# Last stage of a decoder layer: product and addition by token halves, four accumulator pairs in turn, an early root

## The reference

```python
h = h + merged @ w_out                                   # two attention branches, gated
n2 = rmsnorm(h, g_mlp)
h = h + square(relu(n2 @ w_ff1)) @ w_ff2
n3 = rmsnorm(h, g_ple)
h = h + sigmoid(n3 @ w_ple_gate) * (p @ w_ple)           # w_ple: 256 x 1024
return rmsnorm(h, g_final)                               # x * rsqrt(mean(x*x) + 1e-6) * g
```

## Time and profile before

| | |
|---|---|
| median of 3 runs | 1815.67 us (1814.73 to 1817.26) |
| profiled execution, its own time | 1816.49 us |
| its span in the trace | 1814.5 us |
| PE, share of the span | 95% |
| DVE, ACT, POOL | 45%, 31%, 20% |
| mean granted TensorE clock | 0.977 of full speed |

### The profile page before, as it was taken

One profiled execution on the slowest core, in us unless ns is written; L12 is line 12 of the kernel. 1 busy time (PEld: TensorE's weight loads), 2 busy tenths in 40 slices (PEclk: granted clock), 3 DMA queues, 4 the chain that ended last, 5 costly groups with the idle time before them and its releaser, 6 DMA issues.

```text
span 1814.5 us, 21898 instructions
## 1 busy us (share of the span) xinstructions
PE 1727.2 (95%) x8728; PEld 1364.4 (75%) x8728; DVE 808.7 (45%) x1319; ACT 559.5 (31%) x817; POOL 355.5 (20%) x166
## 2 busy tenths in 40 slices
PE   5899989999899999999998999999999999999996
PEld 4568778787556666678887888888888888888885
DVE  7499999901245576554324312122212121215334
ACT  5422322222355566621222212111211111224223
POOL 2212342123100000212211222222222222222220
PEclk8999999999899999999999999999999999999997
DMA  4202123242100020013321111111111111111112
GB/s 149 79 24 58 35 70 99 87 123 65 47 1 1 1 71 1 1 70 139 128 81 35 47 47 47 56 48 46 46 46 46 58 46 46 46 46 41 52 47 92
DMA packets 90324, 103.08 MB, mean 57 GB/s; under 512 B 15920, under 2 KB 82480, under 8 KB 90256
## 3 DMA queue, kind: packets, MB, share of 16 engines
q1 hardware_dynamic: 87504, 92.70, 16.3%
q10 hardware_dynamic: 2592, 9.44, 1.4%
q0 software_dynamic: 160, 0.02, 0.1%
HBM read 86.54 MB, written 13.76 MB: 55 GB/s over the span
## 4 chain that ended last, share of the span: by engine, by line
PE 90%; DVE 4%; ACT 3%; issue 1%; POOL 1%; DMA 0%; ACTq 0%; DVEq 0%; POOLq 0%
PE ps L1466 73%; PE ps L1684 3%; PE ps L1698 3%; PE ps L1649 2%; PE ps L1668 2%; PE ps L1655 2%; PE ps L1563 2%; PE ps L1763 1%; DVE prob_a L1296 1%; DVE sc L1167 1%; PE ps L1625 1%; DVE prob_b L1296 1%; PE ps L1494 0%; PE ps L1827 0%; POOL w_lo L652 0%
## 5 line engine op out<-in xcount | busy, mean ns | idle before, releaser
L652 POOL TENSOR_TENSOR w_lo<-w_raw,w_hi 128x1024 fp32r<-128x1024 f32 x131 | 316.4, 2417 | 1114.4 <-ACT w_hi L736 1114.4
L736 ACT ACTIVATE w_hi<-w_raw 128x1024 fp32r<-128x1024 f32 x131 | 138.7, 1061 | 928.2 <-PE ps L1466 882.0
L1466 PE MATMUL ps<-n_hi,w_hi 128*128 128x512 f32 x1120 | 350.9, 395 | 23.4 <-DVE n_lo L1365 6.6
L1466 PE MATMUL ps<-n_lo,w_hi 128*128 128x512 f32 x1120 | 349.3, 393 | 0.0
L1466 PE MATMUL ps<-n_hi,w_lo 128*128 128x512 f32 x1120 | 348.0, 392 | 0.0
L1466 PEld LDWEIGHTS ps<-n_hi,w_hi 128*128 128x128 f32 x1120 | 212.5, 190 | 71.1 <-issue 11.1
L1466 PEld LDWEIGHTS ps<-n_lo,w_hi 128*128 128x128 f32 x1120 | 213.1, 190 | 44.8
L1466 PEld LDWEIGHTS ps<-n_hi,w_lo 128*128 128x128 f32 x1120 | 212.7, 190 | 44.9
L1394 DVE TENSOR_TENSOR h<-h,ps 128x2048 f32<-128x2048 f32 x32 | 73.2, 2288 | 221.6 <-PE ps L1466 221.6
L1180 DVE TENSOR_SCALAR_CACHE_REDUCE tested<-sc,bar_i 128x384 bf16<-128x384 f32 (+2 forms) x192 | 169.0, 943 | 1.7 <-POOL sc L667 0.6
L1466 PE MATMUL ps<-hid_lo,w_hi 128*128 128x512 f32 x512 | 157.6, 389 | 0.0
(11 more groups left out here) (260 smaller groups left out, 2032.2 us busy)
## 6 DMA issues: line engine op xcount, KB each, us to landing
w_raw<-in_w_ff_dram SPq DMA_DIRECT2D x64, 512.0 KB, 3.5
w_raw<-in_w_in_dram SPq DMA_DIRECT2D x28, 512.0 KB, 3.7
gates_scratch<-stage ACTq DMA_DIRECT2D x16, 512.0 KB, 2.7
sig_ab<-gates_scratch SPq DMA_DIRECT2D x8, 1024.0 KB, 5.9
x_tok<-in_x_dram SPq DMA_DIRECT2D x8, 512.0 KB, 10.5
w_raw<-in_w_out_dram SPq DMA_DIRECT2D x8, 512.0 KB, 4.8
xs<-in_x_dram SPq DMA_DIRECT2D x4, 1024.0 KB, 5.1
w_raw<-in_w_ple_gate_dram SPq DMA_DIRECT2D x8, 512.0 KB, 3.4
```

What stands on the lines that cost most here:

```text
L652: pool.tensor_tensor(w_lo[s][:, :, :], w_raw[s][:, :, :], w_hi[s][:, :, :].bitcast(F32), ALU.subtract).then_inc(lo_ready, 1)
L736: act.activation(w_hi[s][:, :, :], w_raw[s][:, :, :], ACT.Copy).then_inc(hi_ready, 1)
L1466: last = pe.matmul(bank(4 * half + 2 * j + t)[0:w, :], wm, xm[:, t * HALF:(t + 1) * HALF], start=(k == 0 and a), stop=(k == total - 1 and ...
```

## The change

- The product and the addition of round q = 3 are made for tokens 0 to 511 and then for tokens 512 to 1023, four instructions instead of two. `h_final` counts both halves, and PE waits only for the first before it turns tiles 0 to 3, and for the second before tile 4. Between the first product and its addition stands a wait of DVE on its own semaphore (`link`).
- The transposes of tile t go to `fin_bank(t)`: all eight banks as four pairs in turn. Tiles 0 to 3 wait for the two halves to be free of earlier groups, later tiles for the final product of tile t - 4, which a new semaphore `fin_out` counts.
- The output has four buffers, `fin_stage(t)`, both slots of `tmp`, with four `stored` semaphores. The columns of the root are four too, `fin_c`, in the place of `max_c`.
- ACT's squares go to a place of their own, `squares`, over `n2_hi`.
- Right behind the last Sigmoid ACT takes the root of the column `eps_c` into `fin_c[:, 0:1]`, which nothing reads.

```diff
@@ storage and helpers
+        squares = at("squares", NX + 32 * K, [2, S])
+        fin_c = max_c
-        stored = [sem("stored0"), sem("stored1")]
+        stored = [sem(f"stored{b}") for b in range(4)]
+        def fin_bank(t):
+            return bank(4 * ((FIN_GROUP + (t // 2) % 2) % 2) + 2 * (t % 2), 2)
+
+        def fin_stage(t):
+            return tmp[:, (t // 2) % 2, t % 2, :]
@@ SP
             for t in range(TT):
-                g = FIN_GROUP + t
-                freed(sp, g % 2, free_count(g))
-                sp.dma_start(out2[t * P:(t + 1) * P, :], tmp[:, t % 2, 0, :]).then_inc(stored[t % 2], 16)
+                sp.wait_ge(fin_out, t + 1)
+                sp.dma_start(out2[t * P:(t + 1) * P, :], fin_stage(t)).then_inc(stored[t % 4], 16)
@@ ACT
+            act.activation(fin_c[:, 0:1], eps_c, ACT.Sqrt).then_inc(fin_ss, 1)
             for t in range(TT):
-                half = group()
-                if t >= 2:
-                    freed(act, half, free_count(FIN_GROUP + t - 2))
-                act.activation(tmp[:, t % 2, 1, :], bank(4 * half, 2), ACT.Square,
+                group()
+                act.activation(squares[:, t % 2, :], fin_bank(t), ACT.Square,
                                accum_out=ss_c[:, t % 2:t % 2 + 1]).then_inc(fin_ss, 1)
-                act.wait_ge(fin_ss, t + 1)
-                act.activation(rstd_c[:, t % 2:t % 2 + 1], ss_c[:, t % 2:t % 2 + 1], ACT.Sqrt,
+                act.wait_ge(fin_ss, t + 2)
+                act.activation(fin_c[:, t % 4:t % 4 + 1], ss_c[:, t % 2:t % 2 + 1], ACT.Sqrt,
                                bias=eps_c, scale=1.0 / D).then_inc(fin_std, 1)
@@ DVE
                 half = group(1)
-                gate = tmp[:, q % 2, :, :].rearrange("q a n -> q (a n)")
-                pair = h[:, 2 * q:2 * q + 2, :].rearrange("q a n -> q (a n)")
                 dve.wait_ge(gate_fn, q + 1)
-                dve.tensor_tensor(gate, gate, bank(4 * half, 4), ALU.mult).then_inc(psum_free[half], 1)
-                freed(dve, half, free_count(at_.groups - 1))
-                dve.tensor_tensor(pair, pair, gate, ALU.add).then_inc(h_final, 1)
+                for part in [slice(0, S)] if q < 2 * OUT_N - 1 else [slice(0, HALF), slice(HALF, S)]:
+                    gate = tmp[:, q % 2, :, part]
+                    pair = h[:, 2 * q:2 * q + 2, part]
+                    ins = dve.tensor_tensor(gate, gate, ps[:, 4 * half:4 * half + 4, :].rearrange(
+                        "q (a t) n -> q a (t n)", a=2)[:, :, part], ALU.mult)
+                    if part.stop == S:
+                        ins.then_inc(psum_free[half], 1)
+                        freed(dve, half, free_count(at_.groups - 1))
+                    else:
+                        link(ins)
+                    dve.tensor_tensor(pair, pair, gate, ALU.add).then_inc(h_final, 1)
@@ DVE, final norm
-                half, _, _, _ = at_.group()
-                r = rstd_c[:, t % 2:t % 2 + 1]
+                at_.group()
+                r = fin_c[:, t % 4:t % 4 + 1]
                 dve.wait_ge(fin_std, t + 1)
                 link(dve.reciprocal(r, r))
-                if t >= 2:
-                    dve.wait_ge(stored[t % 2], 16 * (t // 2))
-                dve.scalar_tensor_tensor(tmp[:, t % 2, 0, :], bank(4 * half, 2), r, gfin_row[:, :], ALU.mult,
-                                         ALU.mult).then_inc(psum_free[half], 1)
+                if t >= 4:
+                    dve.wait_ge(stored[t % 4], 16 * (t // 4))
+                dve.scalar_tensor_tensor(fin_stage(t), fin_bank(t), r, gfin_row[:, :], ALU.mult,
+                                         ALU.mult).then_inc(fin_out, 1)
@@ PE
-            pe.wait_ge(h_final, 2 * OUT_N)
             for t in range(TT):
-                half = group()
+                if t % 4 == 0:
+                    pe.wait_ge(h_final, 2 * OUT_N + t // 4)
+                if t < 4:
+                    freed(pe, (FIN_GROUP + t // 2) % 2, free_count(FIN_GROUP + t // 2 - 2))
+                else:
+                    pe.wait_ge(fin_out, t - 3)
+                at_.group()
                 for k in range(DT):
-                    last = pe.transpose(bank(4 * half, 2)[:, k * P:(k + 1) * P], h[:, k, t * P:(t + 1) * P], ident[:, :])
+                    last = pe.transpose(fin_bank(t)[:, k * P:(k + 1) * P], h[:, k, t * P:(t + 1) * P], ident[:, :])
                 last.then_inc(turn_done, 1)
```

More of the change, by code:

```diff
@@ L349, in build @@
         fin_std = sem("fin_std")
+        fin_out = sem("fin_out")
         dve_step = sem("dve_step")
@@ L626, in _ @@
             for t in range(TT):
-                g = FIN_GROUP + t
-                freed(sp, g % 2, free_count(g))
-                sp.dma_start(out2[t * P:(t + 1) * P, :], tmp[:, t % 2, 0, :]).then_inc(stored[t % 2], 16)
-            for s in range(2):
-                sp.wait_ge(stored[s], 16 * TT // 2)
+                sp.wait_ge(fin_out, t + 1)
+                sp.dma_start(out2[t * P:(t + 1) * P, :], fin_stage(t)).then_inc(stored[t % 4], 16)
+            for b in range(4):
+                sp.wait_ge(stored[b], 16 * TT // 4)
         @block.gpsimd
```

## The result

The changed kernel takes 1806.51 us, median of 5 runs (1804.84 to 1806.78), against 1816.35 us (1814.73 to 1817.26) for the kernel before in the same comparison: a ratio of 0.9946, 95% interval 0.9933 to 0.9959, or 9.84 us less. Forecast were 10.0 us less and 1805.7 us.

A forecast was written before the change was run, and what follows sets the result against it. The last stage was taken as latency-bound, PE waiting for DVE to read the tile two back. Gains of 3.45 (2.15 + 1.30) and 6.53 us made 10.0, from 1815.67 to 1805.7 us; range 1803.8 to 1808.4.

The forecast's parts named there:

- The bound: Last stage: latency-bound cycle over two accumulator halves, 2.32 us a step; with four pairs DVE sets 1.39, 6.53 us gained.
- Token halves: Last multiply and add split in two: PE's first transpose at 1786.71 instead of 1788.86, 2.15 us gained (2.12 to 2.28).
- Early root: Table load moves behind the last Sigmoid, off the path between first Square and first Sqrt: 1.30 us gained.
- First product: Tile 0's final product on DVE starts at 1790.43, 3.45 us earlier, with PE at its low rate; 1789.5 at high rate.
- Buffers: DVE's new wait on the store of tile t-4: issued 5.6 us earlier, landed 2.6 us after issue, holds nothing back.
- The cover of DVE before the first reciprocal: Second halves leave DVE's queue at about 1789.1, first reciprocal wants it at 1789.3 to 1790.1: only 0.2 us on one side.
- The tail: From the end of the last product to the span's end: store landing 2.6 us after issue, then the close, 3.1 us.
- The effect of PE's rate: If PE is slow for four tiles in the last stage, DVE starves by up to 0.9 us: gain 9.1.
- The upper bound of 1808.4: Upper end of the forecast range in us, taking in A (1807.8) with half a us of the runs' spread.
- A: Rival: PE stays at 1.2 GHz for the whole last stage, 1.69 us a tile; gain 7.9, 1807.8 us; chance 0.10.
- C: Rival: Square and Sqrt alternate tables on ACT, 3.9 us a tile; 10 us slower, 1825.7 us; chance 0.02.
- B: Rival: stores set the last stage's pace or a pipeline step catches, 2.0 us each; gain 5.7, 1810 us; chance 0.07.

The follow-up runs named there:

- 768-column run: Changed kernel with the final product on 768 of 1024 columns of each tile, the stores still moving all 1024: 1804.74 us, ratio to before 0.9937.
- the fillers: Changed kernel with 20 identity transposes, which nothing reads, on TensorE between the last matmul and the first transpose: 1805.26 us, ratio to before 0.9946.
- the three with 47 instruction packets: Changed kernel with 20 identity transposes before tile 0 (1805.26 us), 20 where p is turned (1806.33), or three parts, halved last store and 12 transposes (1805.68).

## Why the prediction was right

*The bound.* Right: the cycle over two halves was the latency of five steps, and with four pairs the chain moved to one engine. The products' distance was forecast as 1.39 from two starts in the earlier trace rows, and it is 1.39 in all seven steps. Only because tile 1 happened to find its inputs ready in the kernel before could that number be read there. The 768-column run shows that it is DVE's.

*Token halves.* First transpose at 2.53 from the multiply, forecast 2.52. Instructions of 1.22 and 1.22 us, forecast 1.22.

*Early root.* The load starts at 1783.25, right behind the Sigmoid, and delays nobody. Alone it gives 1.28 us, forecast 1.30. The Trainium skill, ScalarE: Activation LUTs, section What ACT_TABLE_LOAD costs, has 2.66 us for a switch; by that the first product would have come 1.4 us earlier still. The trace went the way of the row.

*First product.* At 6.28, forecast 6.24, with the low rate that was chosen for it, which all six profiles with PE's gap of 2.57 us show; the other end, full rate, was put 0.9 earlier, and the fillers reached 0.87.

*Buffers.* The wait on the store was costed at nothing because a landing takes 2.6 us and the store was issued 5.6 us earlier. That it costs nothing is right, but the 5.6 is not: four steps of 1.39 lead from the start of one product to the start of another, and a store is issued only when its product ends. Tile 0's store and the product of tile 4, which wants its buffer, in the changed kernel:

```profile
1791.90 10.06 SPq L637 DMA_DIRECT2D out_dram<-tmp  x8
...
1796.15 1.28 DVE L1450 SCALAR_TENSOR_TENSOR tmp<-ps,cols,gfin_row 128x1024 f32<-128x1024 f32 x1
```

That is 4.25 us, so the slack over the landing is 1.6 us and not 3.0. It is the step with the least slack to either side: with two buffers the same sentence costs 3.8 us, and with landings of 4.35 to 4.5 us one of the waits shows.

*The cover of DVE before the first reciprocal.* 0.2 us were forecast for the case of full rate. With the fillers DVE waited 0.34 us there, so it held.

*What was mis-sized.* The tail, 3.20 instead of 3.1 us, since stores in a row land after 2.7. The effect of PE's rate was forecast as up to 0.9 us behind the first product; it was nothing here (40 transposes in 6.25 us, and every product was on time), and 0.24 in the run without halves. The upper bound of 1808.4 is 1808.3 by its own terms, 1807.8 and half a us; nothing hangs on that. The spread of the runs of before was put in part down to PE's rate in this stage; the profiled executions differ by up to 4.5 us before the stage begins, as the start of the multiply shows. The forecast's absolute time lacks 0.8 us, since the median of before was taken from three runs, 1815.67, and is 1816.35 with five; the difference between the kernels was 10.0 forecast and 9.84 measured.

*The rivals.* A (PE low all through) fell at once: the clock was back at 1.00 from 1790 on. C (alternating tables): one load in the stage. B (stores) did not occur in the changed kernel, but the two-buffer run and the three with 47 instruction packets show that it was the rival closest by. The forecast had given it no mechanism of the right kind: not the rate of the stores, which keep 1.33 us a tile, but the time until one lands.

## What to carry to other kernels

A stage in which no engine is full and one cycle repeats is bound by the number of buffers in that cycle: add up the cycle, divide by the buffers, and compare with the slowest single engine. Count every ring that the cycle touches, since four accumulator pairs over two output buffers gave 3.8 us back. Behind the last dense work, cut only as much as gives the next engine its first piece; what is gained there arrives in full at the end so long as the pipeline behind it runs at one engine's pace.

## What the runs showed of the hardware

- Longer code can cost time far from where it stands. 20 instructions more on TensorE came with one more load of 0.02 MB on the instruction queue in the last stage, and with it landings of up to 4.5 us instead of 2.6 to 2.7 and 0.3 us at the end, whether the 20 stood in the stage or 800 us ahead of it. With 12 more the landings reached 4.4 us and the end came 0.6 us later. That the load causes the late landings is not isolated.
- TensorE's clock after 1.5 us of idleness behind dense matmuls was still 1.00 (two kernels), after 2.6 us it was 0.50 for the next 1.98 us of transposes and more (six kernels). The length of the gap alone doesn't settle it: after 4.7 us it was 0.50 in three kernels, and in the one with the pairs alone the first transposes still ran at full rate. The same transposes took 1.98 us for eight at 0.50 and 1.97 us for sixteen at 1.00.
- A store of 256 KB right behind another of 256 KB lands 2.5 us after its issue, one of 512 KB after 2.7.
- A root of one column took 0.29 us with its bias in a column and a scale, and 0.20 us without either.
